# Seven block products per weight chunk: the seventh ahead of the fifth in every pair, and ScalarE's copy of the sixth's sum ahead of the SiLUs

## What is computed

```python
def swiglu(h, w_in, w_out):          # h: 512 x 1024, w_in: 1024 x 5632, w_out: 2816 x 1024
    gu = h @ w_in
    gate, up = gu[..., :D_FF], gu[..., D_FF:]
    return (jax.nn.silu(gate) * up) @ w_out
```

## Time and profile before

| what | value |
|---|---|
| median of 3 runs | 1762.67 us (1759.38 to 1766.97) |
| the profiled execution, own time | 1761.76 us |
| its span, first to last instruction | 1759.9 us |
| TensorE busy | 1746.3 us, 99% of the span, 12738 matmuls |
| VectorE busy | 1332.0 us, 76% |
| ScalarE busy | 834.2 us, 47% |
| mean granted TensorE clock | 0.999 |
| matmuls of line 870 on the chain that ended last | 36% of the span |

### The profile page before, as it was taken

How to read it: one execution, slowest core, us unless ns; L and a number is a source line. 1 busy time by engine, 2 the same in 40 slices (tenths; PEclk the granted TensorE clock), 3 DMA queues, 4 the chain that set the end, 5 groups by cost and what they waited for, 6 DMA issues and landing times.

```text
span 1759.9 us, 31040 instructions
## 1 busy us (share of the span) xinstructions
PE 1746.3 (99%) x12738; PEld 1567.5 (89%) x12745; DVE 1332.0 (76%) x1919; ACT 834.2 (47%) x1389; POOL 31.2 (2%) x63
## 2 busy tenths in 40 slices
PE   9999999999999999999999999999999999999999
PEld 7899899887588899899888998998887988998998
DVE  6899488589858898497588974975888788974964
ACT  5446255355835455255354552553424544552652
POOL 0000000023000000000000000000000000000000
PEclk9999999999999999999999999999999999999999
DMA  6333323322031333323323332232355223322331
GB/s 204 108 128 112 97 97 110 127 69 83 2 108 61 116 113 114 101 97 110 107 66 118 112 113 96 97 117 100 113 157 147 97 80 112 120 97 96 111 106 48
DMA packets 74439, 183.22 MB, mean 104 GB/s; under 512 B 23713, under 2 KB 30513, under 8 KB 74305
## 3 DMA queue, kind: packets, MB, share of 16 engines
q1 hardware_dynamic: 72128, 179.02, 31.1%
q0 software_dynamic: 1600, 1.52, 0.3%
q10 hardware_dynamic: 576, 0.79, 0.1%
HBM read 174.35 MB, written 6.29 MB: 103 GB/s over the span
## 4 chain that ended last, share of the span: by engine, by line
PE 97%; DVE 1%; DMA 1%; issue 1%; ACT 0%; SPq 0%; ACTq 0%; DVEq 0%
PE bank L870 36%; PE bank L529 16%; PE bank L531 16%; PE bank L530 16%; PE bank L622 4%; PE bank L627 2%; PE bank L931 1%; PE bank L963 1%; PE bank L907 1%; PE bank L556 1%; PE bank L1029 1%; PE bank L548 1%; PE bank L946 0%; PE bank L596 0%; PE bank L597 0%
## 5 line engine op out<-in xcount | busy, mean ns | idle before, releaser
L529 PE MATMUL bank<-a_hi,w_hi 128*128 128x512 f32 (+1 forms) x912 | 334.8, 367 | 1.1 <-issue 1.1
L530 PE MATMUL bank<-a_lo,w_hi 128*128 128x512 f32 (+1 forms) x912 | 332.8, 365 | 0.0
L531 PE MATMUL bank<-a_hi,w_lo 128*128 128x512 f32 (+1 forms) x912 | 332.8, 365 | 0.0
L1184 ACT ACTIVATE w_hi<-w_raw 128x1024 fp32r<-128x1024 f32 x192 | 202.9, 1059 | 198.4 <-DVE w_raw L1564 159.9
L870 PE MATMUL bank<-x_hi,w_hi 128*128 128x256 f32 x1024 | 290.2, 283 | 0.0
L870 PE MATMUL bank<-x_lo,w_hi 128*128 128x256 f32 x1024 | 289.7, 283 | 0.0
L870 PE MATMUL bank<-x_hi,w_lo 128*128 128x256 f32 x1024 | 289.6, 283 | 0.0
L1556 DVE TENSOR_TENSOR w_lo<-w_raw,w_hi 128x1024 fp32r<-128x1024 f32 x192 | 234.7, 1222 | 27.4 <-ACT w_hi L1184 26.3
L1544 DVE TENSOR_TENSOR w_lo<-w_raw,w_hi 128x1024 fp32r<-128x1024 f32 x142 | 173.7, 1223 | 90.8 <-ACT w_hi L1133 90.4
L1133 ACT ACTIVATE w_hi<-w_raw 128x1024 fp32r<-128x1024 f32 x142 | 146.7, 1054 | 196.1 <-PE bank L531 183.5
L870 PE MATMUL bank<-raw_forms_hi,w_lo 128*128 128x256 f32 x768 | 215.8, 281 | 0.0
(11 more groups left out here) (250 smaller groups left out, 2914.2 us busy)
## 6 DMA issues: line engine op xcount, KB each, us to landing
w_raw<-stream SPq DMA_DIRECT2D x312, 512.0 KB, 3.3
h_resid<-xT SPq DMA_DIRECT2D x8, 256.0 KB, 6.1
qT<-stream SPq DMA_DIRECT2D x8, 256.0 KB, 6.1
u_scratch<-V SPq DMA_DIRECT2D x8, 256.0 KB, 3.3
a_lo<-u_scratch SPq DMA_DIRECT2D x8, 256.0 KB, 3.0
qT<-z_scratch SPq DMA_DIRECT2D x8, 256.0 KB, 5.2
outT<-h_resid SPq DMA_DIRECT2D x10, 128.0 KB, 1.9
z_scratch<-kT SPq DMA_DIRECT2D x2, 256.0 KB, 4.2
```

What stands on the lines that cost most here:

```text
L529: nc.tensor.matmul(out, lw[0], lx[0], start=first, stop=False)
L530: nc.tensor.matmul(out, lw[0], lx[1], start=False, stop=False)
L531: return nc.tensor.matmul(out, lw[1], lx[0], start=False, stop=last)
L1184: nc.scalar.activation(units_to(w_hi, pair, split), units_from(pair, split), ACT.Copy).then_inc(s_uhi, 1)
```

## The change

In `product_order` every pair now runs UP7 ahead of UP5. In ScalarE's `pairs` the copy of the sum after UP6 now stands, in all pairs but the first of a group, ahead of `silu_first`. In the first pair it stays where it was. Two waits of ScalarE name UP5 in the place of UP7, as the last product of the pair.

```diff
@@ product_order
         order += [(p, UP6)]
         if p:
             order += [(p - 1, UP3)]
-        order += [(p, UP7), (p, UP5)] if p == FAST - 1 else [(p, UP5), (p, UP7)]
+        order += [(p, UP7), (p, UP5)]
     return order + [(FAST - 1, UP4), (FAST - 1, UP3)]
@@ block.scalar, pairs
                     if more_pairs:
                         if i:
-                            act.wait_ge(s_up, multiplied(pair - 1, UP7))
+                            act.wait_ge(s_up, multiplied(pair - 1, UP5))
                         else:
                             act.wait_ge(s_mm, n0)
                         units_hi(ahead, 1)
                         if i == 0:
                             seen_of(pair, UP6, 1)
                         units_hi(ahead, 2)
                     else:
-                        down_hi(n0 + 1, 1, pair - 1, UP7)
+                        down_hi(n0 + 1, 1, pair - 1, UP5)
+                    if i:
+                        seen_of(pair, UP6, 1)
                     silu_first(pair)
                     if i:
                         silu_second(pair - 1)
-                        seen_of(pair, UP6, 1)
```

## The result

The changed kernel took 1769.82 us (median of 20 runs, 1766.16 to 1775.36) against 1763.67 us (20 runs, 1759.38 to 1768.80): ratio 1.0036, 95% interval 1.0027 to 1.0046, so 6.1 us slower. The forecast was 6.1 us; that the two agree to 0.1 us is in part luck, since the interval reaches from 4.8 to 8.1 us.

A forecast was written before the change was run, and what follows sets the result against it. The prediction took TensorE, busy for 99% of the span, as the bound. A loss of 6.56 us less a gain of 0.5 us gave +6.1 us on 1762.67 us, so 1768.8 us, range 1764.5 to 1775 us.

The forecast's parts named there:

- The wait in the first pair: First pair of each group: UP7's weight load waits for ScalarE's copy after UP6, 0.82 us late, 6.56 us over eight groups.
- The weights pulled ahead: First pair: UP7's weights might load before the copy ends, costing 0.70 us a group, 5.6 us in all; not adopted.
- The other pairs at 0, and 0.06 us back in the second: Pairs after the first: the earlier copy leaves no pause, cost 0; the second pair's 0.06 us go, 0.5 us gained.
- The copy and the delayed SiLUs at 0: ScalarE: the moved copy does not hold up middle pairs' SiLUs; the last pair's wait has 1 us to spare, cost 0.
- UP5 last at 0: End of a pair: with UP5 as last product, VectorE's `second_up`, which needs it, starts no later, cost 0.
- What the copy behind the SiLUs would have done: Middle pairs, copy not moved: it would end at 151.10 and UP7 come at 151.21 instead of 150.12.
- Not slower: Rival: the down projection behind each group takes up the loss, 1762.7 us less at most 0.5 us; chance 0.04.
- Late copies in the middle pairs: Rival: a weight split delays the copy, 0.45 us in each of 6 pairs, 21.6 us, 1790.4 us in all; chance 0.05.
- The clock: Rival: TensorE's clock falls at each new pause, 1.44 us lost per group, 11.5 us, 1780.3 us in all; chance 0.05.

The follow-up runs named there:

- The last experiment: The changed kernel, with ScalarE's third weight split ahead of the copy after UP6 in a group's first pair: 1772.11 us, ratio 1.0048 to the kernel before.
- the first pair covered: The changed kernel, with UP5 back between UP6 and UP7 in the first pair of a group: 1761.76 us, ratio 0.9996 to the kernel before.
- the copy alone: The kernel before, with its order of products kept and only ScalarE's copy moved ahead of the SiLUs: 1761.27 us against 1762.42, ratio 0.9995.
- the loop through UP3 opened: The order alone, plus VectorE's third split of weight rests ahead of its wait for UP3: 1777.80 us, ratio 1.0091 to the kernel before.
- The order alone: The changed kernel's order of products in all pairs, with ScalarE's copy left behind both SiLUs: 1780.14 us, ratio 1.0104 to the kernel before.
- the first four experiments: The four runs measured against the kernel before at 1762.42 us: the first pair covered, the copy alone, The order alone and The last experiment.

## Why the prediction was right, point by point

- *The wait in the first pair, 0.82 us a group.* The load was 0.81 us late. The way from the copy's end to the load is 0.11 to 0.12 us, at this wait and at every late load of UP7 in the other runs, as in the earlier trace rows, the row of the same wait. The last experiment shows that the copy's end sets it. That every matmul behind the load moves by as much was off by a little: they come 0.79 us later.
- *The weights pulled ahead.* By the rule of the Trainium skill ("TensorE: Matmul & The Clock Gate", section "Step-by-step: what each phase is for") the weights of UP7 might have been loaded before the copy was done, for 0.70 us a group. The load at 111.40 comes after the copy's end at 111.28, as in the earlier trace rows, so the rule did not make this wait cheaper.
- *The other pairs at 0, and 0.06 us back in the second.* Right: no other pair of the eight groups has a pause, and a group is longer by the first pair's 0.79 us than the 79.97 us that it lasts with that pair covered. By the traces the sum is 8 x 0.79 us lost less 8 x 0.05 us gained, 5.9 us, where 6.56 less 0.5 us had been forecast.
- *The copy and the delayed SiLUs at 0.* Right, shown by the copy alone and by the last pair's rows. A detail was off: I expected the SiLUs of middle pairs where they were. They start 0.65 us earlier against TensorE (150.75, where 150.13 + 1.27 = 151.40 was due), since the pause in the first pair does not hold VectorE up: its `first_gate` of the second pair comes at 120.57 instead of 120.04, only 0.53 us later, while TensorE is 1.27 us later.
- *UP5 last at 0.* Right while the copy is early. With the copy late, UP5's place does seem to cost: the 0.09 us in each middle pair of the experiment in which the loop through UP3 was opened.
- *What the copy behind the SiLUs would have done.* Here a step failed, though it carried no term: I set the copy's end of 151.10 against the due time 150.12, as if VectorE's times were fixed and each middle pair would lose 1.09 us. The order alone loses 0.7 us once, in the second pair, and then on average about 0.2 us in each middle pair. TensorE's first delay puts it behind VectorE for good; after that only loops longer than 10.0 us cost.
- *The rivals.* Not slower: the down projection kept its 43.54 us. Late copies in the middle pairs: none. The clock: 1.00 in all eight groups, even with a pause of 1.22 us. The Trainium skill ("TensorE: Matmul & The Clock Gate", section "HAM oscillation — how this bites in real kernels") tells of a kernel that waits for data in every round, longer than it computes, and loses its clock each time; the pauses here, 0.81 or 1.22 us once in a group of 81 us, show nothing of the kind. One reading was incomplete: in the trace before, the granted clock is at 0.50 also in the last 0.5 us of the span, where TensorE has no work left; no time hangs on it.

The best version is the one with the first pair covered, or the copy alone: both are as fast as the kernel before within what can be measured, and 0.4% faster than the change.

## What to carry to other kernels

A cover that hides a copy in the middle of a loop can be missing in its first round, where the work of the round before does not exist; write out the order of the first round when you swap two steps. Price such a wait as the chain from the producer's end over the copy to the next weight load, and multiply by how often the first round comes. When the waiting engine is the bound and the others are not, a delay is paid once, unless a loop over several engines is longer than the bound's own round; look for that loop before you multiply a delay by the rounds.

## What the runs showed that I had not expected

In the profiled execution after the change the granted clock fell in the layer norm, where the one before kept 1.00 (windows 1342.00 to 1356.00 of the kernel after, columns as in the earlier trace rows):

```profile
1342.00:1352.00 10.00, 8.70 (x293) 7.69 (x285) 8.26 (x14) 1.90 (x3) 0.00 (x0) 1.00 0.62 141
...
1350.00:1354.00 4.00, 4.00 (x78) 3.05 (x76) 2.35 (x7) 2.02 (x4) 0.00 (x0) 0.79 0.94 235
1354.00:1356.00 2.00, 2.00 (x18) 1.86 (x18) 0.00 (x0) 0.09 (x1) 0.00 (x0) 0.50 1.03 374
```

The value 0.50 is the level of 1.2 GHz. The code of this stretch is the same in both kernels. TensorE had been busy for 8.70 of the 10 us ahead of the fall, and for 8.40 of 10 us at the same place behind the sixth group in the kernel before, which kept its clock:

```profile
1337.26:1347.26 10.00, 8.40 (x310) 7.42 (x303) 8.50 (x14) 1.90 (x3) 0.00 (x0) 1.00 0.57 135
```

So the same stretch can keep the clock in one execution and lose it in another. In the seven profiled executions of this document, the stretch between the sixth and the seventh group lasted 321.9 to 322.4 us in the four with a fall (the change, the first pair covered, the later copy, the loop through UP3 opened) and 319.4 to 320.7 us in the three without (the kernel before, the copy alone, the order alone). The fall comes without the change's wait (first pair covered), and the wait without the fall (order alone). The kernel before loses clock in other executions too: over the 23 of the first four experiments' comparison its mean granted clock went from 0.996 (1767.13 us) to 1.000 (1760.20 us), and over the 20 of the changed kernel from 0.995 (1775.36 us) to 1.000 (1766.16 us). This is why windows, and not single spans, told the 5.9 us of the change from the rest.
